# Storing pairs of k-tiles of split weights woven, so that a weight load steps by 8 bytes

## The chip, the cores and the metric

The kernel runs on one core of a Trainium2 chip. The metric is the device time of one execution in microseconds (us).

## What is computed

One decoder layer over 280 token columns: 16 meta tokens, 256 prompt tokens and 8 sample tokens. Nearly all of the arithmetic is in four matrix products in fp32 (D = 2048, DFF = 5632):

```python
z = rmsnorm(x, norm1_g) @ w_in            # 2048 x 16400
x = x + mix @ w_out                       # 2048 x 2048
up = causal_dwconv(rmsnorm(x) @ w_up)     # 2048 x 11264
x = x + (silu(up[..., D_FF:]) * up[..., :D_FF]) @ w_down   # 5632 x 2048
```

Between them stand a short convolution, an mLSTM over 8 heads, gates and norms. Beside the two outputs the kernel returns the new states.

## The kernel before

Activations lie transposed in SBUF: 128 features on the partitions, the tokens along the free axis. Each product is made of strips. A strip is 128 output features; it is accumulated in one PSUM bank (`strip0` to `strip3`, used in turn) over all k-tiles of 128 input features. A strip is made of two or three **units** of at most KU = 8 k-tiles; a unit's weights are one DMA of 128 x 1024 fp32 (512 KB).

fp32 accuracy comes from splitting. `w_hi` is the weight rounded to fp32r, the type with which TensorE makes a product in one pass, and `w_lo` is the rest, `w_raw - w_hi`. The activations are split in the same way (`xh`, `xl` for the norms' outputs, `mh`, `ml` for the mixed heads, `hh`, `hl` for the hidden layer). A unit is 24 matmuls: for each k-tile `w_hi` with `xh` and `w_hi` with `xl` (line 1497), then for each k-tile `w_lo` with `xh` (line 1502). The weights are the stationary operand, so each of these matmuls has its own load of 128 x 128 weights into the array (LDWEIGHTS, shown as engine PEld), and the activations of 264 to 280 token columns stream past them.

The weights go through a ring of RING = 4 slots in each of `w_raw`, `w_hi` and `w_lo`:

- SP (line 379) loads unit u + 4 into `w_raw` when VectorE has made `w_lo` of unit u (`lo_done`).
- ScalarE (line 704, `split_hi`) writes `w_hi` of unit u + 4 when its weights have landed and TensorE has finished unit u (`unit_used`).
- VectorE (line 963, `split_lo`) writes `w_lo` after `hi_done`.
- TensorE waits for `hi_done`, runs the 16 matmuls of the high part, waits for `lo_done`, and runs the 8 of the low part (`unit`, `strip`).

For the first four units VectorE (lines 1009 and 1016), GpSimd (lines 484 and 488) and ScalarE (lines 725 and 726) share that work, in order to start TensorE early (`first_hi`, `first_lo_part`). The order on each engine is written out by hand; loops run over heads, strips and pairs of feature tiles. VectorE also takes every strip out of PSUM (line 972), and VectorE, ScalarE and GpSimd make the convolutions, gates and states.

In each slot k-tile k lies in columns 128 k to 128 k + 127, one word of 4 bytes beside the other.

Of the kernel before, what the change touches and what calls it, by code (L numbers as in the profile page):

```python
# [6 lines left out]
def hybrid_decoder_step(nc, ins, outs, scratch_rows, scratch_v, scratch_q):  # L7
# [10 lines left out]
    f32, f32r = mybir.dt.float32, mybir.dt.float32r  # L18
    ALU, ACT = mybir.AluOpType, mybir.ActivationFunctionType
# [7 lines left out]
    P = 128  # L27
# [12 lines left out]
    NT = TP + NS  # L40
# [24 lines left out]
    KU = 8  # L65
# [37 lines left out]
    with ctx:  # L103
        def sb(name, shape, dt=f32):
            return ctx.enter_context(nc.sbuf_tensor(name, shape, dt))

        def sem(name):
            return ctx.enter_context(nc.semaphore(name))
# [5 lines left out]
        w_raw = sb("w_raw", [P, RING, KU * P])  # L114
        w_hi = sb("w_hi", [P, RING, KU * P], f32r)
        w_lo = sb("w_lo", [P, RING, KU * P], f32r)
# [172 lines left out]
        bank = [ctx.enter_context(nc.psum_tensor(f"strip{i}", [P, 512], f32)) for i in range(RING)]  # L289
# [4 lines left out]
        hi_done = sem("hi_done")  # L294
# [6 lines left out]
        half_hi, first_lo, mp_done, bias_done = sem("half_hi"), sem("first_lo"), sem("mp_done"), sem("bias_done")  # L301
# [55 lines left out]
        def out_of(s):  # L357
            return s + 1 + RING

        def col(c, j):  # L360
            return vecs[:, bass.ds(c * KT + j, 1)]

# [103 lines left out]
        def _(g):  # L466
# [14 lines left out]
            g.memset(gws[:, :, :].bitcast(f32), 0.0).then_inc(gw_split, 1)  # L481
            g.wait_ge(hi_done, 2)
            g.wait_ge(first_lo, 1)
            g.tensor_tensor(w_lo[:, 2, :], w_raw[:, 2, :], w_hi[:, 2, :].bitcast(f32), ALU.subtract)\
             .then_inc(first_lo, 1)
            for i, u in enumerate((1, 3)):
                g.wait_ge(hi_done, i + 3)
                g.tensor_tensor(w_lo[:, u, :], w_raw[:, u, :], w_hi[:, u, :].bitcast(f32), ALU.subtract)\
                 .then_inc(lo_done, 2)

            g.wait_ge(gates_in, 16)
# [152 lines left out]
            for m in range(KT):  # L644
# [5 lines left out]
                if m < NQ:  # L650
                    p = slice(m * Q, (m + 1) * Q)
# [48 lines left out]
        def _(act):  # L700
            def split_hi(u, slot, n16):
                act.wait_ge(unit_landed[slot], n16)
                act.wait_ge(unit_used, u + 1)
                act.activation(w_hi[:, slot, :], w_raw[:, slot, :], ACT.Copy).then_inc(hi_done, 1)  # L704

            def step(n, per, base_u, i):

                u4 = n * per + (base_u + i + RING)
                split_hi(u4, i % RING, n * (16 * per // RING) + 16 * ((base_u + i) // RING + 2))
# [9 lines left out]
            for k in range(KT):  # L719
                act.wait_ge(x_turned, k + 1)  # L720
                act.activation(xh[:, k, :], x_bank[k % 6][:, 0:NT], ACT.Copy, scale=vecs[:, k:k + 1])\
                 .then_inc(xh_done, 1)
                if k == 3:
                    act.wait_ge(unit_landed[0], 16)
                    act.activation(w_hi[:, 0, 0:KU * P // 2], w_raw[:, 0, 0:KU * P // 2], ACT.Copy).then_inc(half_hi, 1)
                    act.activation(w_hi[:, 0, KU * P // 2:], w_raw[:, 0, KU * P // 2:], ACT.Copy).then_inc(hi_done, 1)
                for kept in (k - 2, k) if k % 4 == 3 else ():
                    act.wait_ge(xl_done, kept + 1)
                    act.activation(xres[:, kept, :], x_bank[kept % 6][:, 0:NT], ACT.Copy).then_inc(x_copied, 1)
                if k == 7:  # L730
                    act.wait_ge(hi_done, 2)
                    split_hi(1, 1, 16)
# [227 lines left out]
        def _(v):  # L960
            def split_lo(u, slot):
                v.wait_ge(hi_done, u + 1)
                v.tensor_tensor(w_lo[:, slot, :], w_raw[:, slot, :], w_hi[:, slot, :].bitcast(f32),  # L963
                                ALU.subtract).then_inc(lo_done, 1)

            def step(n, per, base_u, i):
                split_lo(n * per + (base_u + i + RING), i % RING)
# [31 lines left out]
            for k in range(KT):  # L999
                v.wait_ge(xh_done, k + 1)  # L1000
                v.scalar_tensor_tensor(out=xl[:, k, :], in0=x_bank[k % 6][:, 0:NT], scalar=vecs[:, k:k + 1],
                                       in1=xh[:, k, :].bitcast(f32), op0=ALU.mult, op1=ALU.subtract)\
                                        .then_inc(xl_done, 1)
                if k % 2 == 1:
                    v.tensor_copy(xres[:, k - 1, :], x_bank[(k - 1) % 6][:, 0:NT]).then_inc(x_kept, 1)
                if k == 3:
                    v.wait_ge(half_hi, 1)
                    v.wait_ge(hi_done, 1)
                    v.tensor_tensor(w_lo[:, 0, :], w_raw[:, 0, :], w_hi[:, 0, :].bitcast(f32), ALU.subtract)\
                     .then_inc(first_lo, 1)  # L1010
                if k in (3, 11):
                    u = 2 if k == 3 else 3
                    v.wait_ge(unit_landed[u], 16)
                    if k == 11:
                        v.wait_ge(hi_done, 3)
                    v.tensor_scalar(w_hi[:, u, :], w_raw[:, u, :], 1.0, None, ALU.mult).then_inc(hi_done, 1)
            v.wait_ge(lo_done, RING + 4)
            v.wait_ge(ssq_done, 3)
            v.wait_ge(msq_clear, 1)
# [353 lines left out]
        def _(pe):  # L1373
# [43 lines left out]
            def first_hi(s, lo, hi):  # L1417
                c0 = C0 if s == 0 else 0
                for k in range(lo, hi):
                    if s == 0 and k == 0:  # L1420
                        pe.wait_ge(half_hi, 1)
                    elif k % KU == 0 or (s == 0 and k == 4):
                        pe.wait_ge(hi_done, 1 + s + 2 * (k // KU))
                    pe.wait_ge(xl_done, k + 1)
                    w = slice(k % KU * P, (k % KU + 1) * P)
                    for t, xt in enumerate((xh, xl)):
                        mm = pe.matmul(bank[s][:, 0:NT - c0], w_hi[:, 2 * s + k // KU, w], xt[:, k, c0:NT],  # L1427
                                       start=(k == 0 and t == 0), stop=False)
                return mm

            def first_lo_part(s, lo, hi, last=False):
                c0 = C0 if s == 0 else 0
                h = lo // KU
                if h == 0:
                    pe.wait_ge(first_lo, s + 1)
                else:
                    pe.wait_ge(lo_done, RING + 2 * (s + 1))
                for k in range(lo, hi):
                    pe.wait_ge(xh_done, k + 1)
                    mm = pe.matmul(bank[s][:, 0:NT - c0], w_lo[:, 2 * s + h, (k - h * KU) * P:(k - h * KU + 1) * P],  # L1440
                                   xh[:, k, c0:NT], start=False, stop=(last and k == KT - 1))
                return mm

# [7 lines left out]
            turn_x(0, 4)  # L1451
            warm(6)
            first_hi(0, 0, 4)
            turn_x(4, 8)
            first_lo_part(0, 0, 4)
            first_hi(1, 0, 4)
            first_hi(0, 4, 6)
            first_lo_part(0, 4, 8)
            first_hi(0, 6, 8).then_inc(unit_used, 1)
            first_lo_part(1, 0, 4)  # L1460
            turn_x(8, 12)
            first_hi(1, 4, 8)
# [24 lines left out]
            def unit(u, slot, b, k0, kk, rh, rl, c0, c1, first, last, waits=(), frees=1):  # L1487


                pe.wait_ge(hi_done, u + 1)  # L1490
                for k in range(kk):
                    for at_k, sm, value in waits:
                        if at_k == k:
                            pe.wait_ge(sm, value)
                    w = slice(k * P, (k + 1) * P)
                    for t, xt in enumerate((rh, rl)):
                        pe.matmul(bank[b][:, 0:c1 - c0], w_hi[:, slot, w], xt[:, k0 + k, c0:c1],  # L1497
                                  start=(first and k == 0 and t == 0), stop=False)
                pe.wait_ge(lo_done, u + 1 + RING)
                for k in range(kk):  # L1500
                    w = slice(k * P, (k + 1) * P)
                    mm = pe.matmul(bank[b][:, 0:c1 - c0], w_lo[:, slot, w], rh[:, k0 + k, c0:c1],  # L1502
                                   start=False, stop=(last and k == kk - 1))
                if frees:
                    mm.then_inc(unit_used, frees)
# [112 lines left out]
            def out_unit(q, h, waits, frees):  # L1618
                unit(U_B + 2 * q + h, 2 * q + h, q, h * KU, KU, mh, ml, 0, NM, h == 0, h == 1, waits, frees)
# [109 lines left out]
```

## Time and profile before

| | |
|---|---|
| median of 3 runs | 1712.78 us (1712.42 to 1715.47) |
| the profiled execution, own time | 1712.32 us |
| its span, first to last instruction | 1710.6 us |
| TensorE matmul busy (PE) | 1699.2 us, 99% |
| TensorE weight load busy (PEld) | 1692.9 us |
| VectorE (DVE) / ScalarE (ACT) / GpSimd (POOL) busy | 1200.8 / 766.4 / 475.1 us |
| mean granted TensorE clock | 0.998 |

The span is what the trace covers; 1.7 us lie around it. Records of matmuls and loads overlap each other, since a matmul is recorded until its last result is out, so their busy time says only that TensorE never rests. What one matmul costs is the distance from its start to the next one's start, called the pitch below.

### The profile page before, as it was taken

The numbers are of one execution on the slowest core, as the hardware profiler recorded it, in microseconds if no ns is written. First come the engines' busy times: TensorE is split into PE (matmuls) and PEld (weight loads), VectorE is DVE, ScalarE is ACT, GpSimd is POOL, SyncE is SP. The second block draws the span as 40 slices with busy tenths as digits, with TensorE's granted clock in tenths as the row PEclk, the third lists the DMA queues.
The fourth block names the chain that finished last, engine by engine and source line by source line (L and its number), as shares of the span: only waits on it lengthen the run. The fifth ranks groups of instructions, "written<-read, shape, count | busy, mean of one in ns | idle before, by whom it ended". The sixth has DMA issues, their size and how long they took to land.

```text
span 1710.6 us, 37176 instructions
## 1 busy us (share of the span) xinstructions
PE 1699.2 (99%) x13726; PEld 1692.9 (99%) x13726; DVE 1200.8 (70%) x1902; ACT 766.4 (45%) x914; POOL 475.1 (28%) x501
## 2 busy tenths in 40 slices
PE   9999999999999999999999999999999999999997
PEld 8999999999999999999999999999999999999997
DVE  5875958667595766759688877777555777777554
ACT  6545345354443535344444554544333434333443
POOL 4522414242141424215333222222000222222220
PEclk9999999999999999999999999999999999999999
DMA  8787786868778586877866666666666666666663
GB/s 209 176 235 191 203 213 156 223 159 230 188 196 212 155 225 162 232 184 195 192 174 185 186 175 180 179 176 172 183 181 182 180 176 179 174 182 175 182 178 119
DMA packets 591165, 318.80 MB, mean 186 GB/s; under 512 B 17684, under 2 KB 585988, under 8 KB 588988
## 3 DMA queue, kind: packets, MB, share of 16 engines
q1 hardware_dynamic: 578564, 292.99, 63.7%
q10 hardware_dynamic: 10448, 21.57, 4.9%
q0 software_dynamic: 2064, 2.92, 0.8%
q8 instruction: 72, 1.18, 0.3%
q14 instruction: 17, 0.14, 0.0%
HBM read 305.09 MB, written 12.78 MB: 186 GB/s over the span
## 4 chain that ended last, share of the span: by engine, by line
PE 99%; ACT 0%; DVE 0%; POOL 0%; issue 0%; ACTq 0%; POOLq 0%
PE strip L1497 63%; PE strip L1502 32%; PE aux L1375 1%; PE aux L1383 0%; PE strip L1427 0%; PE aux L1555 0%; PE aux L1447 0%; PE strip L1440 0%; PE aux L1585 0%; PE aux L1584 0%; PE aux L1598 0%; PE strip L1375 0%; PE aux L1589 0%; PE aux L1582 0%; PE aux L1590 0%; PE aux L1591 0%
## 5 line engine op out<-in xcount | busy, mean ns | idle before, releaser
L963 DVE TENSOR_TENSOR w_lo<-w_raw,w_hi 128x1024 fp32r<-128x1024 f32 x556 | 718.8, 1296 | 317.6 <-ACT w_hi L704 317.0
L704 ACT ACTIVATE w_hi<-w_raw 128x1024 fp32r<-128x1024 f32 x557 | 586.5, 1059 | 766.0 <-PE strip L1502 730.9
L1497 PE MATMUL strip<-xh,w_hi 128*128 128x268 f32 (+2 forms) x3424 | 863.8, 286 | 0.0
L1497 PE MATMUL strip<-xl,w_hi 128*128 128x268 f32 (+2 forms) x3424 | 862.9, 286 | 0.0
L1497 PEld LDWEIGHTS strip<-xh,w_hi 128*128 128x128 f32 x3424 | 644.9, 188 | 0.2
L1497 PEld LDWEIGHTS strip<-xl,w_hi 128*128 128x128 f32 x3424 | 644.5, 188 | 0.0
L1502 PE MATMUL strip<-xh,w_lo 128*128 128x268 f32 (+2 forms) x3424 | 495.2, 287 | 0.0
L1502 PEld LDWEIGHTS strip<-xh,w_lo 128*128 128x128 f32 x3424 | 451.9, 189 | 0.4 <-DVE w_lo L963 0.4
L1497 PE MATMUL strip<-hh,w_hi 128*128 128x264 f32 x704 | 176.2, 285 | 0.0
L1497 PE MATMUL strip<-hl,w_hi 128*128 128x264 f32 x704 | 174.8, 283 | 0.0
L675 POOL TENSOR_TENSOR gg<-sg,cz 128x264 f32<-128x264 f32 x44 | 57.2, 1301 | 415.1 <-ACT sg L918 415.1
L1497 PEld LDWEIGHTS strip<-hh,w_hi 128*128 128x128 f32 x704 | 132.4, 188 | 0.0
L1497 PEld LDWEIGHTS strip<-hl,w_hi 128*128 128x128 f32 x704 | 132.3, 188 | 0.0
L678 POOL TENSOR_TENSOR hid<-gg,cz 128x264 f32<-128x264 f32 x44 | 73.5, 1671 | 102.2 <-DVE cz L1308 102.2
L1502 PE MATMUL strip<-hh,w_lo 128*128 128x264 f32 x704 | 100.6, 283 | 0.0
L1502 PEld LDWEIGHTS strip<-hh,w_lo 128*128 128x128 f32 x704 | 91.5, 188 | 0.0
L1497 PE MATMUL strip<-ml,w_hi 128*128 128x266 f32 x256 | 64.8, 287 | 0.0
L1497 PE MATMUL strip<-mh,w_hi 128*128 128x266 f32 x256 | 64.7, 287 | 0.0
L615 POOL TENSOR_TENSOR so<-so,sbm 128x266 f32<-128x266 f32 x16 | 20.6, 1287 | 138.9 <-ACT sbm L876 138.9
L972 DVE TENSOR_TENSOR zs<-strip,rbc 128x266 f32<-128x266 f32 x88 | 37.9, 431 | 26.6 <-PE strip L1502 26.6
L606 POOL TENSOR_TENSOR c_st<-c_st,kv 128x512 f32<-128x512 f32 x32 | 52.1, 1628 | 5.4 <-ACT c_st L859 3.4
L1300 DVE SCALAR_TENSOR_TENSOR cz<-zs,vecs,cz 128x256 f32<-128x256 f32 x88 | 42.7, 485 | 12.9 <-DVE cz L1297 1.8
(324 smaller groups left out, 1331.5 us busy)
## 6 DMA issues: line engine op xcount, KB each, us to landing
w_raw<-in_w_in SPq DMA_DIRECT2D x256, 512.0 KB, 4.4
w_raw<-in_w_up SPq DMA_DIRECT2D x176, 512.0 KB, 4.1
w_raw<-in_w_down SPq DMA_DIRECT2D x64, 512.0 KB, 3.9
w_raw<-in_w_out SPq DMA_DIRECT2D x32, 512.0 KB, 4.4
w_raw<-in_w_down SPq DMA_DIRECT2D x32, 384.0 KB, 3.3
out<-c_st ACTq DMA_DIRECT2D x8, 1024.0 KB, 7.1
c_st<-in_state_mlstm_C ACTq DMA_DIRECT2D x7, 1024.0 KB, 10.6
rb<-scratch_rows ACTq DMA_DIRECT2D x8, 270.0 KB, 5.1
```

The source lines that it names most:

```text
L606: g.tensor_tensor(c_p, c_p, kv[:, :, :], ALU.add).then_inc(c_updated, 1)
L615: g.tensor_tensor(so[:, :], so[:, :], sbm[:, :], ALU.mult).then_inc(p_gate, 1)
L675: g.tensor_tensor(gg[:, :], sg[:, :], cz[:, 0, :], ALU.mult).then_inc(gg_done, 1)
L678: g.tensor_tensor(hid[:, :], gg[:, :], cz[:, 1, :], ALU.mult).then_inc(hid_done, 1)
L704: act.activation(w_hi[:, slot, :], w_raw[:, slot, :], ACT.Copy).then_inc(hi_done, 1)
L963: v.tensor_tensor(w_lo[:, slot, :], w_raw[:, slot, :], w_hi[:, slot, :].bitcast(f32), ALU.subtract).then_inc(lo_done, 1)
L972: v.tensor_tensor(out, bank[b][:, c0 - from_c:c0 - from_c + width], rbc[:, c0:c0 + width], ALU.mult).then_inc(evacuated, 1)
L1300: v.scalar_tensor_tensor(out=cz[:, z, 0:SEQ], in0=zs[:, z, 1:1 + SEQ], scalar=wcol[1], in1=cz[:, z, 0:SEQ], op0=ALU.mult, op1=ALU.add)\
L1375: return pe.transpose(out, in_, ident[0:k, 0:k])
L1497: pe.matmul(bank[b][:, 0:c1 - c0], w_hi[:, slot, w], xt[:, k0 + k, c0:c1], start=(first and k == 0 and t == 0), stop=False)
L1502: mm = pe.matmul(bank[b][:, 0:c1 - c0], w_lo[:, slot, w], rh[:, k0 + k, c0:c1], start=False, stop=(last and k == kk - 1))
```

## The change

`w_hi` and `w_lo` are laid out in another order inside a slot. Two neighbouring k-tiles share 256 columns: the even k-tile has the even words, the odd one the odd words. The writers (ScalarE, VectorE, and GpSimd for the first units) read `w_raw` as before and write through a view whose innermost step is two words (`woven`); where they read `w_hi` for the subtraction, they read it through the same view. TensorE's loads of weights take 128 columns two words apart (`wk`). `w_raw` and the DMAs, the activations, the streams past the weights, the semaphores and the order of the instructions are as before: on TensorE and SP each instruction stands where it stood, on ScalarE, VectorE and GpSimd the splitting instructions have the shape 128x4x2x128 in place of 128x1024. The hunks left out are the same edit at ScalarE's first unit and in `first_hi` and `first_lo_part`.

```diff
--- before.py
+++ after.py
@@ -357,6 +357,15 @@
         def out_of(s):
             return s + 1 + RING
 
+        def raw(slot, k0=0, k1=KU):
+            return w_raw[:, slot, k0 * P:k1 * P].rearrange("p (a j n) -> p a j n", j=2, n=P)
+
+        def woven(t, slot, k0=0, k1=KU):
+            return t[:, slot, k0 * P:k1 * P].rearrange("p (a n j) -> p a j n", j=2, n=P)
+
+        def wk(t, slot, k):
+            return t[:, slot, k // 2 * 2 * P + k % 2:(k // 2 + 1) * 2 * P:2]
+
         def col(c, j):
             return vecs[:, bass.ds(c * KT + j, 1)]
 
...
@@ -481,11 +490,11 @@
             g.memset(gws[:, :, :].bitcast(f32), 0.0).then_inc(gw_split, 1)
             g.wait_ge(hi_done, 2)
             g.wait_ge(first_lo, 1)
-            g.tensor_tensor(w_lo[:, 2, :], w_raw[:, 2, :], w_hi[:, 2, :].bitcast(f32), ALU.subtract)\
+            g.tensor_tensor(woven(w_lo, 2), raw(2), woven(w_hi, 2).bitcast(f32), ALU.subtract)\
              .then_inc(first_lo, 1)
             for i, u in enumerate((1, 3)):
                 g.wait_ge(hi_done, i + 3)
-                g.tensor_tensor(w_lo[:, u, :], w_raw[:, u, :], w_hi[:, u, :].bitcast(f32), ALU.subtract)\
+                g.tensor_tensor(woven(w_lo, u), raw(u), woven(w_hi, u).bitcast(f32), ALU.subtract)\
                  .then_inc(lo_done, 2)
 
             g.wait_ge(gates_in, 16)
@@ -701,7 +710,7 @@
             def split_hi(u, slot, n16):
                 act.wait_ge(unit_landed[slot], n16)
                 act.wait_ge(unit_used, u + 1)
-                act.activation(w_hi[:, slot, :], w_raw[:, slot, :], ACT.Copy).then_inc(hi_done, 1)
+                act.activation(woven(w_hi, slot), raw(slot), ACT.Copy).then_inc(hi_done, 1)
 
             def step(n, per, base_u, i):
 
...
@@ -960,7 +969,7 @@
         def _(v):
             def split_lo(u, slot):
                 v.wait_ge(hi_done, u + 1)
-                v.tensor_tensor(w_lo[:, slot, :], w_raw[:, slot, :], w_hi[:, slot, :].bitcast(f32),
+                v.tensor_tensor(woven(w_lo, slot), raw(slot), woven(w_hi, slot).bitcast(f32),
                                 ALU.subtract).then_inc(lo_done, 1)
 
             def step(n, per, base_u, i):
@@ -1006,14 +1015,14 @@
                 if k == 3:
                     v.wait_ge(half_hi, 1)
                     v.wait_ge(hi_done, 1)
-                    v.tensor_tensor(w_lo[:, 0, :], w_raw[:, 0, :], w_hi[:, 0, :].bitcast(f32), ALU.subtract)\
+                    v.tensor_tensor(woven(w_lo, 0), raw(0), woven(w_hi, 0).bitcast(f32), ALU.subtract)\
                      .then_inc(first_lo, 1)
                 if k in (3, 11):
                     u = 2 if k == 3 else 3
                     v.wait_ge(unit_landed[u], 16)
                     if k == 11:
                         v.wait_ge(hi_done, 3)
-                    v.tensor_scalar(w_hi[:, u, :], w_raw[:, u, :], 1.0, None, ALU.mult).then_inc(hi_done, 1)
+                    v.tensor_scalar(woven(w_hi, u), raw(u), 1.0, None, ALU.mult).then_inc(hi_done, 1)
             v.wait_ge(lo_done, RING + 4)
             v.wait_ge(ssq_done, 3)
             v.wait_ge(msq_clear, 1)
...
@@ -1492,14 +1500,12 @@
                     for at_k, sm, value in waits:
                         if at_k == k:
                             pe.wait_ge(sm, value)
-                    w = slice(k * P, (k + 1) * P)
                     for t, xt in enumerate((rh, rl)):
-                        pe.matmul(bank[b][:, 0:c1 - c0], w_hi[:, slot, w], xt[:, k0 + k, c0:c1],
+                        pe.matmul(bank[b][:, 0:c1 - c0], wk(w_hi, slot, k), xt[:, k0 + k, c0:c1],
                                   start=(first and k == 0 and t == 0), stop=False)
                 pe.wait_ge(lo_done, u + 1 + RING)
                 for k in range(kk):
-                    w = slice(k * P, (k + 1) * P)
-                    mm = pe.matmul(bank[b][:, 0:c1 - c0], w_lo[:, slot, w], rh[:, k0 + k, c0:c1],
+                    mm = pe.matmul(bank[b][:, 0:c1 - c0], wk(w_lo, slot, k), rh[:, k0 + k, c0:c1],
                                    start=False, stop=(last and k == kk - 1))
                 if frees:
                     mm.then_inc(unit_used, frees)

```

## Rows read from the trace of the kernel before

**Rows 1.** The page, parts 1 and 2: busy us, share, instructions; TensorE's clock.
```profile
PE 1699.2 (99%) x13726; PEld 1692.9 (99%) x13726; DVE 1200.8 (70%) x1902; ACT 766.4 (45%) x914; POOL 475.1 (28%) x501
...
PEclk9999999999999999999999999999999999999999
```

**Rows 2.** The page, part 4: shares of the chain that ended last, by engine.
```profile
PE 99%; ACT 0%; DVE 0%; POOL 0%; issue 0%; ACTq 0%; POOLq 0%
```

**Rows 3.** The page, part 5: groups of strip matmuls, for their counts.
```profile
L1502 PE MATMUL strip<-xh,w_lo 128*128 128x268 f32 (+2 forms) x3424 | 495.2, 287 | 0.0
...
L1502 PE MATMUL strip<-hh,w_lo 128*128 128x264 f32 x704 | 100.6, 283 | 0.0
...
L1497 PE MATMUL strip<-ml,w_hi 128*128 128x266 f32 x256 | 64.8, 287 | 0.0
```

**Rows 4.** Windows: stretch, length, each engine busy (count), clock, DMA share, GB/s.
```profile
129.00:147.00 18.00, 18.00 (x142) 18.00 (x142) 9.14 (x12) 6.37 (x6) 2.13 (x7) 1.00 0.96 227
156.00:190.00 34.00, 34.00 (x277) 34.00 (x277) 27.28 (x36) 18.84 (x29) 20.01 (x19) 1.00 0.52 133
195.00:229.00 34.00, 34.00 (x280) 34.00 (x279) 22.88 (x34) 13.00 (x15) 10.05 (x10) 1.00 0.90 240
826.00:916.00 90.00, 90.00 (x729) 90.00 (x728) 70.79 (x96) 36.90 (x46) 36.83 (x48) 1.00 0.75 188
925.00:1175.00 250.00, 250.00 (x2034) 250.00 (x2033) 198.74 (x385) 126.31 (x129) 58.34 (x42) 1.00 0.62 178
1185.00:1305.00 120.00, 120.00 (x993) 120.00 (x992) 62.47 (x62) 47.75 (x45) 0.00 (x0) 1.00 0.64 184
```

**Rows 5.** Timeline: start us, length us, engine, line, shape; loads and half-rate matmuls.
```profile
13.55 0.47 PEld L1375 LDWEIGHTS strip<-ident,x_tok 128*128 128x128 f32 x4
...
90.89 0.31 PEld L1585 LDWEIGHTS aux<-pt,v 128*128 128x128 f32 x2
91.00 0.41 PE L1585 MATMUL aux<-pt,v 128*128 128x144 f32 x2
...
92.70 0.53 PEld L1598 LDWEIGHTS aux<-sel,sacc 128*128 128x128 f32 x4
```

**Rows 6.** Lines L1375, L1447, L1497, L1585: ns min/median/max, first and last start.
```profile
L1375 PEld LDWEIGHTS strip<-ident,x_tok x4: 139/140/142, 13.5 to 13.9; 128*128 128x128 f32 x4
...
L1447 PEld LDWEIGHTS aux<-xh,gws x16: 167/168/174, 27.9 to 31.7; 128*104 128x104 f32 x16
...
L1497 PEld LDWEIGHTS strip<-xh,w_hi x3424: 186/188/193, 33.0 to 1566.4; 128*128 128x128 f32 x191
...
L1585 PEld LDWEIGHTS aux<-pt,v x32: 191/192/192, 90.9 to 793.2; 128*128 128x128 f32 x32
```

**Rows 7.** Timeline of PE: consecutive matmuls of one shape.
```profile
1300.11 0.28 PE L1497 MATMUL strip<-hh,w_hi 128*128 128x264 f32 x1
1300.22 0.29 PE L1497 MATMUL strip<-hl,w_hi 128*128 128x264 f32 x1
1300.36 0.28 PE L1497 MATMUL strip<-hh,w_hi 128*128 128x264 f32 x1
1300.47 0.29 PE L1497 MATMUL strip<-hl,w_hi 128*128 128x264 f32 x1
```

**Rows 8.** The page, part 5: splitting on VectorE and ScalarE, and a short eviction.
```profile
L963 DVE TENSOR_TENSOR w_lo<-w_raw,w_hi 128x1024 fp32r<-128x1024 f32 x556 | 718.8, 1296 | 317.6 <-ACT w_hi L704 317.0
L704 ACT ACTIVATE w_hi<-w_raw 128x1024 fp32r<-128x1024 f32 x557 | 586.5, 1059 | 766.0 <-PE strip L1502 730.9
...
L972 DVE TENSOR_TENSOR zs<-strip,rbc 128x266 f32<-128x266 f32 x88 | 37.9, 431 | 26.6 <-PE strip L1502 26.6
```

**Rows 9.** Lines L963 and L1016 by themselves: ns min/median/max, first and last start.
```profile
L963 DVE TENSOR_TENSOR w_lo<-w_raw,w_hi x556: 1181/1224/2891, 31.6 to 1689.8; 128x1024 fp32r<-128x1024 f32 x186
...
L1016 DVE TENSOR_SCALAR w_hi<-w_raw x2: 680/682/683, 13.0 to 21.5; 128x1024 fp32r<-128x1024 f32 x2
```

More of the change, by code:

```diff
@@ L724, in _ @@
                     act.wait_ge(unit_landed[0], 16)
-                    act.activation(w_hi[:, 0, 0:KU * P // 2], w_raw[:, 0, 0:KU * P // 2], ACT.Copy).then_inc(half_hi, 1)
-                    act.activation(w_hi[:, 0, KU * P // 2:], w_raw[:, 0, KU * P // 2:], ACT.Copy).then_inc(hi_done, 1)
+                    act.activation(woven(w_hi, 0, 0, KU // 2), raw(0, 0, KU // 2), ACT.Copy).then_inc(half_hi, 1)
+                    act.activation(woven(w_hi, 0, KU // 2), raw(0, KU // 2), ACT.Copy).then_inc(hi_done, 1)
                 for kept in (k - 2, k) if k % 4 == 3 else ():
@@ L1424, in first_hi @@
                     pe.wait_ge(xl_done, k + 1)
-                    w = slice(k % KU * P, (k % KU + 1) * P)
                     for t, xt in enumerate((xh, xl)):
-                        mm = pe.matmul(bank[s][:, 0:NT - c0], w_hi[:, 2 * s + k // KU, w], xt[:, k, c0:NT],
+                        mm = pe.matmul(bank[s][:, 0:NT - c0], wk(w_hi, 2 * s + k // KU, k % KU), xt[:, k, c0:NT],
                                        start=(k == 0 and t == 0), stop=False)
@@ L1439, in first_lo_part @@
                     pe.wait_ge(xh_done, k + 1)
-                    mm = pe.matmul(bank[s][:, 0:NT - c0], w_lo[:, 2 * s + h, (k - h * KU) * P:(k - h * KU + 1) * P],
+                    mm = pe.matmul(bank[s][:, 0:NT - c0], wk(w_lo, 2 * s + h, k - h * KU),
                                    xh[:, k, c0:NT], start=False, stop=(last and k == KT - 1))
```

## The prediction, made before the changed kernel was run

> **What bounds the kernel now.** I read the page first. TensorE is busy for 99% of the span and its clock is granted in full in every slice [rows 1], which is its level of 2.4 GHz. The chain of work that ended last is TensorE's own for 99% [rows 2]. So the span is a sum of matmul pitches (start to start), and the change can act in two ways: it alters the pitch, or it slows a writer of weights so much that TensorE must wait.
>
> The strips have 13,248 matmuls. The lines of the loops show 3424 + 704 + 256 = 4384 for one of the three products of a k-tile [rows 3], so 13,152, and the first units add 4 x 24 = 96. For their pitch I asked for windows that hold strips and little else [rows 4]. A window also counts the matmul or two that began before it, so I add one matmul's length, 0.28 us [rows 7], before I divide: 128.8 ns for 280 columns (129:147), 123.8 and 122.4 for 268 (156:190 and 195:229), 123.8 and 123.0 for 266 (826:916 and 925:1175), 121.1 for 264 (1185:1305). At one column per cycle of 2.4 GHz these streams take 116.7, 111.7, 110.8 and 110.0 ns. So every strip matmul costs 11 to 13 ns more than its stream, about 11.8 on average. That is 13,248 x 11.8 = 156 us of the span, and the only part of it that a layout of weights can touch.
>
> **What the excess is.** Three readings.
> (a) It is not the other engines or the DMAs: of the two windows with 268 columns the one with a DMA share of 0.52 has 123.8 ns and the one with 0.90 has 122.4 [rows 4].
> (b) It is not the length of the load. A load of 104 columns is recorded at 168 ns and one of 128 at 188 [rows 6], so 20/24 = 0.83 ns per column, and 128 columns take 107 ns. Four loads whose matmuls stream only 8 columns follow each other in (0.53 - 0.19)/3 = 0.113 us [rows 5, 6]. So a load fits into the 121 to 129 ns of a pitch, but with only some 10 ns to spare.
> (c) Where the stream runs at two cycles per column, the excess is hardly there, though the loads are as many. Two matmuls of 144 columns: loads (0.31 - 0.19) = 0.12 us apart, against 2 x 144/2.4 = 120 ns. Transposes of 128 columns: (0.47 - 0.14)/3 = 0.11 us, against 107 [rows 5, 6]. I take 2.5 ns, and it may be 0 to 5.
> Besides, gaps between matmuls of one shape in one strip are uneven: 0.11, 0.14, 0.11 us [rows 7].
>
> My reading, an inference and not shown by a row: the load of the next weights and the stream of the present matmul read SBUF at the same time, and when both want the same part of it the stream stalls. At full rate the stream has no free cycles to make up for it; at half rate it has. In bytes per partition the stream now advances at 4 / 0.417 = 9.6 B/ns and the load at 4 / 0.83 = 4.8 B/ns, so the stream overtakes the load again and again within a matmul.
>
> **The change part by part.**
> *Loads.* 13,248 loads step by 8 bytes instead of 4. If a load keeps its 0.83 ns per column, it now advances at 9.6 B/ns, as fast as the stream. Then the two keep a fixed distance. If they collide at the start, one stall puts them apart for the rest of the matmul. So the stalls should mostly go. At best the pitch falls to the stream plus 2.5 ns: 9.3 ns less for each, 13,248 x 9.3 = 123 us. The floor set by the load itself, 107 to 113 ns, is just reached at 264 columns (110 + 2.5). I take 8 of the 9.3 ns, since one or two stalls at the start of a matmul should remain: 13,248 x 8 = 106 us. The other end: the trace before has no load that steps, so nothing excludes that a step costs time. A load of twice as many SBUF lines could double the conflicts (+9.3 ns), or double its length (second and fourth rival).
>
> *Writers.* 557 splits on ScalarE (1059 ns) and 556 on VectorE (1296 ns) now write with a step of two words, and VectorE reads `w_hi` so [rows 8]. VectorE's subtraction costs (1224 - 431)/(1024 - 266) = 1.05 ns per element, with its median of 1224 ns [rows 9] and an eviction of 266 elements at 431 [rows 8]: one element per step, nothing packed that a stride could break. I cost them at nothing. What hides them is the ring: ScalarE waited 730.9 us for TensorE before its splits, and VectorE 317.0 us for ScalarE [rows 8], and a unit's weights are due only when three more units of 24 x 0.123 = 2.95 us have run. With pitches shorter by 8 ns a unit lasts 24 x 0.115 = 2.76 us. VectorE's 1200.8 us [rows 1] then fill 75% of 1606 us, so it does not become the bound.
>
> *Start.* VectorE makes `w_hi` of units 2 and 3 in 0.68 us each for 1024 elements [rows 9], faster than one element per 1.05 ns (1.07 us). A step may take this away: 2 x 0.4 = 0.8 us, bounded by nothing and by twice that, at a place where GpSimd and TensorE wait for it. I add 1 us.
>
> *Unchanged.* DMAs, instruction order and waits. The DMA share is 0.96 at worst while states are loaded [rows 4]; units that come 7% sooner press on that place, and `w_raw` may land late there. Eight such stretches at up to 1 us give 0 to 8 us; I take 1.
>
> **Sum.** Against the profiled execution's own 1712.3 us (the median of the runs is 1712.8, the same within 0.03%): -106 + 1 + 1 = -104, so **1608 us**.
>
> **A rule that speaks against it.** By rows, the excess is 11 to 13 ns beside full-rate streams and 0 to 5 beside half-rate ones, and this is what I build on. The Trainium skill, "TensorE: Matmul & The Clock Gate", section "Step-by-step: what each phase is for", says that TensorE has two independent read ports into SBUF and that loading the next weights takes no read bandwidth from the running matmul. By that there is no conflict to remove. "Advanced Engine Details and Errata", section "SBUF Cachelines", adds that lines are 16 bytes and that two hits per line suffice for full speed: a step of 8 bytes of fp32 has just two. By both the time would stay at 1712; no run here shows a stepped load yet.
>
> **The rivals.**
> 1. *The excess is a fixed cost of changing weights at full rate and the layout does not matter.* Pitch 121 to 129 as before, 1712 to 1713 us. For it: the excess is near 12 ns at 264 and at 280 columns [rows 4]. Against it: the uneven gaps [rows 7], and 266 columns costing 123.8 in one stage and 123.0 in another [rows 4]. The rules above give the same time. 18%.
> 2. *Slower: conflicts grow with the lines that a load touches.* 128 columns now span 1024 bytes instead of 512. Twice the conflicts is +9.3 ns, 13,248 x 9.3 = +123, so 1836 us. It decides as soon as the stalls per matmul exceed today's; at half of that growth the time is 1774. For it: a faster load has less idle time between its reads. Against: only if the fixed distance does not hold. 21%.
> 3. *Slower: the writers become the bound.* If a stepped write or read took two steps per element, VectorE's 556 subtractions would take 1.07 us more each: 1200.8 + 595 = 1796 us of work, more than the span. With some idle time left, 1800 to 1850. ScalarE at 766.4 + 590 would still fit. For it: only that no large stepped write is in the trace. 5%.
> 4. *Slower: the load takes twice as long.* 2 x 107 + 6 = 220 ns per matmul instead of 123: 13,248 x 97 = +1285, so about 3000 us. For it: the load has only some 10 ns to spare. 6%.
>
> **How the numbers follow.** My forecast has 50%; its own range goes from 1585 (all 123 us, with the small losses at nothing) to 1695 (a seventh of it). The predicted time is its 1608. The range that should hold 8 in 10 must reach the first two rivals: 1585 to 1840. Outside lie the fourth rival, some of the third and the upper part of the second. A measurement of this kernel tells 0.2%, about 3.4 us, from no change. Faster: 50%. Within 0.2%: the first rival, 18%. Slower: 21 + 5 + 6 = 32%.
>
> **What would show it.** In the profile of the changed kernel: windows in the same stages with about 115 ns per matmul instead of 123, gaps in a strip that are even, loads still recorded near 188 ns, splits near 1059 and 1224 ns, TensorE still at 99%. A load recorded at 290 ns or so would be the fourth rival. Splits near 2.3 us with TensorE waiting for `w_lo` would be the third. Gaps above 123 ns with loads at 188 would be the second. Unchanged pitches to within 0.3 ns would be the first. The prediction is wrong if the excess is not a conflict between load and stream, or if equal speed makes the conflict permanent instead of ending it.

## The result, and the profile after

The changed kernel takes 1735.99 us (median of 4 runs, 1735.41 to 1737.38) where the one before takes 1712.9. The ratio is 1.0131, with a 95% interval of 1.0119 to 1.0143: it is slower by 23 us, and clear of the 0.2% that a measurement can tell.

The page of the changed kernel: the clock and TensorE's share are as in [rows 1], ScalarE's busy time is up by 51 us, and VectorE's (-1.6 us) and GpSimd's (+3.5 us) hardly move.

```profile
PE 1723.2 (99%) x13726; PEld 1716.8 (99%) x13726; DVE 1199.2 (69%) x1902; ACT 817.1 (47%) x914; POOL 478.6 (28%) x501
...
L713 ACT ACTIVATE w_hi<-w_raw 128x1024 fp32r<-128x1024 f32 x557 | 638.3, 1153 | 746.2 <-PE strip L1508 701.3
```

TensorE's own waits after (engine and line that waited, for whom: us in total, times, longest). This is all of them, none is for weights, and the kernel before has the same three (2.1, 1.2 and 0.3 us); so the time went into the pitch:

```profile
PE aux L1392 <- POOL a L484: 2.1, 1, 2.1
PE aux L1700 <- DVE rfs L999: 1.2, 1, 1.2
PE aux L1689 <- ACT sqs L906: 0.3, 1, 0.3
```

Windows of the changed kernel in the stages of [rows 4], moved to where those stages now lie (stretch, length, busy and count of PE, PEld, DVE, ACT, POOL, clock, DMA share, GB/s):

```profile
132.00:148.00 16.00, 16.00 (x125) 16.00 (x125) 7.36 (x11) 6.07 (x6) 1.36 (x7) 1.00 0.98 221
158.00:192.00 34.00, 34.00 (x276) 34.00 (x275) 27.06 (x37) 19.86 (x30) 20.15 (x19) 1.00 0.53 136
198.00:232.00 34.00, 34.00 (x276) 34.00 (x275) 22.43 (x33) 13.97 (x15) 10.06 (x10) 1.00 0.88 238
835.00:925.00 90.00, 90.00 (x722) 90.00 (x722) 68.58 (x96) 39.69 (x45) 40.01 (x47) 1.00 0.75 185
935.00:1185.00 250.00, 250.00 (x1989) 250.00 (x1988) 194.59 (x379) 131.50 (x126) 56.46 (x42) 1.00 0.61 174
1200.00:1320.00 120.00, 120.00 (x979) 120.00 (x978) 60.67 (x60) 51.00 (x45) 0.00 (x0) 1.00 0.63 181
```

With one matmul's 0.28 us added as in the prediction, the pitches are 130.2 ns at 280 columns (128.7 before by [rows 4], where the prediction wrote 128.8), 124.2 at 268 in both stages (123.8 and 122.4), 125.0 and 125.8 at 266 (123.8 and 123.0), and 122.9 at 264 (121.1). So the cost is uneven, from 0.4 to 2.8 ns. The mean over the starts of all strip matmuls in the two traces rises from 123.4 to 125.1 ns, that is by 1.74 ns, and 13,248 x 1.74 = 23 us. The span grew by 24.1 us (1710.6 to 1734.7); the other 1.2 us lie at the start, see below. The loads are recorded 8 ns longer than in [rows 6]. VectorE's subtractions keep their median of [rows 9] within 2 ns and its two copies within 4 ns (ns min/median/max):

```profile
L1504 PEld LDWEIGHTS strip<-xh,w_hi x3424: 193/196/203, 34.3 to 1588.6; 128*128 128x128 f32 x191
...
L972 DVE TENSOR_TENSOR w_lo<-w_raw,w_hi x556: 1181/1226/2884, 33.0 to 1713.9; 128x1024 fp32r<-128x1024 f32 x186
...
L1025 DVE TENSOR_SCALAR w_hi<-w_raw x2: 682/686/689, 14.2 to 22.7; 128x1024 fp32r<-128x1024 f32 x2
```

### The profile page after: what moved, and what is told of

The parts are those of the page before. It is cut to its first block, busy times and chain, and to the rows that moved or that the text cites. A ratio compares the mean times of both kernels' runs of the same rounds, so it can differ in the third digit from the quotient of the medians.

```text
span 1734.7 us, 37176 instructions
## 1 busy us (share of the span) xinstructions
PE 1723.2 (99%) x13726; PEld 1716.8 (99%) x13726; DVE 1199.2 (69%) x1902; ACT 817.1 (47%) x914; POOL 478.6 (28%) x501
## 4 chain that ended last, share of the span: by engine, by line
PE 94%; DVE 2%; ACT 1%; issue 1%; DMA 1%; POOL 0%; DVEq 0%; ACTq 0%; POOLq 0%
PE strip L1504 61%; PE strip L1508 31%; DVE w_lo L972 1%; PE aux L1384 1%; PE aux L1561 0%; DMA rb<-scratch_rows 0%; DMA scratch_rows<-rows 0%; ACT sq_junk L748 0%; PE aux L1591 0%; PE aux L1590 0%; PE aux L1604 0%; PE aux L1597 0%; PE aux L1588 0%; PE aux L1596 0%; PE aux L1595 0%
## 5 line engine op out<-in xcount | busy, mean ns | idle before, releaser
L713 ACT ACTIVATE w_hi<-w_raw 128x1024 fp32r<-128x1024 f32 x557 | 638.3, 1153 | 746.2 <-PE strip L1508 701.3
L1504 PE MATMUL strip<-xh,w_hi 128*128 128x268 f32 (+2 forms) x3424 | 878.2, 290 | 0.0
L1504 PE MATMUL strip<-xl,w_hi 128*128 128x268 f32 (+2 forms) x3424 | 875.7, 288 | 0.0
L1504 PEld LDWEIGHTS strip<-xl,w_hi 128*128 128x128 f32 x3424 | 674.5, 197 | 0.0
L1504 PEld LDWEIGHTS strip<-xh,w_hi 128*128 128x128 f32 x3424 | 671.4, 196 | 0.2
L1508 PEld LDWEIGHTS strip<-xh,w_lo 128*128 128x128 f32 x3424 | 458.3, 196 | 0.3 <-DVE w_lo L972 0.3
L1504 PEld LDWEIGHTS strip<-hh,w_hi 128*128 128x128 f32 x704 | 137.9, 196 | 0.0
L1504 PEld LDWEIGHTS strip<-hl,w_hi 128*128 128x128 f32 x704 | 137.5, 195 | 0.0
L1504 PEld LDWEIGHTS strip<-ml,w_hi 128*128 128x128 f32 x256 | 50.6, 198 | 0.0
```

Source lines behind the costliest of these rows:

```text
L713: act.activation(woven(w_hi, slot), raw(slot), ACT.Copy).then_inc(hi_done, 1)
L1504: pe.matmul(bank[b][:, 0:c1 - c0], wk(w_hi, slot, k), xt[:, k0 + k, c0:c1], start=(first and k == 0 and t == 0), stop=False)
L1508: mm = pe.matmul(bank[b][:, 0:c1 - c0], wk(w_lo, slot, k), rh[:, k0 + k, c0:c1], start=False, stop=(last and k == kk - 1))
```

## The experiments

All start from the kernel before, except the one with the writers, which starts from the changed one. Of each edit the lines that matter are shown; the same edit is made where `w_lo` is loaded, and a stepped or step-0 load also in the first four units. None of these kernels computes the layer: they leave out work or multiply other data. Differences below are between a kernel's median and that of the kernel before in the same session (1713.5 to 1714.5 us).

### Which half of the change costs

Loads alone:

```diff
+        def wk(t, slot, k):
+            return t[:, slot, k // 2 * 2 * P + k % 2:(k // 2 + 1) * 2 * P:2]
-                        pe.matmul(bank[b][:, 0:c1 - c0], w_hi[:, slot, w], xt[:, k0 + k, c0:c1],
+                        pe.matmul(bank[b][:, 0:c1 - c0], wk(w_hi, slot, k), xt[:, k0 + k, c0:c1],
```

> Only the loads step by 8 bytes; the writers store plain as before (so each load takes every second word of two k-tiles, and the products are other ones). If the 23 us come from the stepped loads, it shows all of them: 1735 to 1737 us, loads at 196 ns, ScalarE's split back at 1059 ns. If they come from the stepped writes on ScalarE and VectorE that disturb TensorE's reads, it is back at 1712 to 1714 us with loads at 188 ns. A mixture would lie between.

Writers alone (the changed kernel with `wk` reading 128 neighbouring columns):

```diff
-            return t[:, slot, k // 2 * 2 * P + k % 2:(k // 2 + 1) * 2 * P:2]
+            return t[:, slot, k * P:(k + 1) * P]
```

> The complement: the writers store woven, the loads are plain again (the products are other ones). If the loads are the cause: 1712 to 1714 us, loads at 188 ns, ScalarE's split still at 1156 ns, which the ring hides. If the writes are the cause: 1735 us.

Loads alone: 1736.31 us, ratio 1.0127 (1.011 to 1.0144). Writers alone: 1713.93 us, ratio 1.0 (0.999 to 1.0009). All of the cost in the pitch is in the loads. The woven write does make ScalarE's split longer (1146 ns instead of 1059), and the ring hides it. Page of the kernel with loads alone, then of the one with writers alone (the last columns: busy us, mean ns, idle before it):

```profile
L1498 PEld LDWEIGHTS strip<-xh,w_hi 128*128 128x128 f32 x3424 | 671.4, 196 | 0.2
L707 ACT ACTIVATE w_hi<-w_raw 128x1024 fp32r<-128x1024 f32 x557 | 586.5, 1059 | 792.2 <-PE strip L1502 755.6 <-DMA w_raw<-in_w_in 18.7 <-issue 7.3
```

```profile
L1504 PEld LDWEIGHTS strip<-xh,w_hi 128*128 128x128 f32 x3424 | 644.9, 188 | 0.2
L713 ACT ACTIVATE w_hi<-w_raw 128x1024 fp32r<-128x1024 f32 x557 | 634.4, 1146 | 723.2 <-PE strip L1508 681.2 <-DMA w_raw<-in_w_in 20.9 <-issue 8.3
```

### A longer step, and none

```diff
+            return t[:, slot, k // 4 * 4 * P + k % 4:(k // 4 + 1) * 4 * P:4]     # step 16 bytes
+            return t[:, slot, k * P:k * P + 1].broadcast_to([P, P])              # step 0
```

> Loads step by 16 bytes, one word of each 16, writers plain (other products). Theory A, the cost grows with the number of 16-byte lines that a load touches (32, 64, now 128): recorded load at least 196 + 16 = 212 ns, excess above the stream another 3 to 4 ns or more, 1780 us or slower; if one hit per line costs the load a full second access, its length doubles and the time is above 2500 us. Theory B, any step costs the same fixed amount: 1735 to 1740 us. Theory C, the length of the path through SBUF banks matters by chance of addresses: anything from 1700 to 1760 us.

> All 128 columns of a load are the same word (step 0; other products): the load touches a single line. Theory A (load and stream disturb each other by the lines the load reads): the excess over the stream falls from 11.8 to near 2.5 ns, 1590 to 1620 us. Rival (a fixed cost of full-rate matmuls with a load each): 1712 us, no change.

Step of 16 bytes: 3183.44 us, ratio 1.8569 (1.8538 to 1.86). The window of 1695 to 2170 (266 columns) and the loads of that kernel:

```profile
1695.00:2170.00 475.00, 475.00 (x2030) 475.00 (x2030) 200.25 (x386) 124.93 (x127) 57.85 (x42) 1.00 0.32 94
```

```profile
L1498 PEld LDWEIGHTS strip<-xh,w_hi 128*128 128x128 f32 x3424 | 1132.7, 331 | 0.2
```

The load is 331 - 188 = 143 ns longer, and the pitch is 475.28/2030 = 234 ns here, and 233 and 234 ns in the stages with 280 and 268 columns: the load has become the bound. With one word used of each 16 bytes, the loads follow each other in 234 ns where plain ones did in 0.113 us [rows 5]; with two words used (8 bytes) a load is recorded 8 ns longer. The Trainium skill, "Advanced Engine Details and Errata", section "SBUF Cachelines", says that two hits per line suffice and that a line for each access costs; the cliff between 8 and 16 bytes agrees, but two hits were not quite free for loads.

Step 0: 1698.34 us, ratio 0.991 (0.9893 to 0.9926), 16 us less where the theory behind my prediction wanted 95 to 125. A load that touches a single line leaves the excess at some 10.5 ns. The window of 918 to 1160 gives 242.28/1991 = 121.7 ns, against 123.0 before and a stream of 110.8:

```profile
918.00:1160.00 242.00, 242.00 (x1991) 242.00 (x1991) 194.55 (x380) 123.50 (x126) 57.61 (x41) 1.00 0.62 180
```

So most of the excess does not go with the lines that the load reads. That theory (A in the expectation) fell here, and so did the rival beside it, which had no change at all.

### Streams that stay in one place

```diff
-                                  xt[:, k0 + k, c0:c1],
+                                  xt[:, k0 + k, c0:c0 + 1].broadcast_to([P, c1 - c0]),
```

> Plain loads; in the strips' matmuls of the loops each stream reads one word over and over (step 0; other products). With the load's lines already shown to matter little (step 0 there took 16 us off), what remains of the excess of about 11 ns per matmul is either the stream's own reading of SBUF, in which case the pitch falls to the stream plus 2.5 ns and the time to 1590 to 1600 us, or a fixed cost of one load and one full-rate matmul each, in which case it stays within 1695 to 1715 us.

> The same with loads that step by 8 bytes. If stepped loads cost by conflicts with the stream's reads, the step adds nothing here: equal to the run with plain loads and one-word streams, within 3 us, though the load may still be recorded at 196 ns. If the stepped load by itself is longer and holds up the next matmul, it adds the same 22 us as with real streams.

Plain loads: 1618.16 us, ratio 0.9443 (0.9427 to 0.9459), 95 us less. Stepped loads: 1651.58 us, ratio 0.9636 (0.962 to 0.9652), 33 us more than the plain ones. The plain one is slower than the 1590 to 1600 us expected, though its pitch is as expected (below), because TensorE, now faster, waits for others: 8.8 us for `w_lo` (22 times) and once 4.4 us for `hl`, where TensorE in the kernel before waits for neither, and the granted clock is 0.97 in the stretch with that longest wait (1120:1235). So read the pitches rather than the total. Two windows of each, with 280 and with 266 columns (plain, then stepped):

```profile
127.00:141.00 14.00, 14.00 (x120) 14.00 (x119) 6.24 (x9) 4.51 (x5) 2.62 (x7) 1.00 1.00 232
...
785.00:870.00 85.00, 85.00 (x753) 85.00 (x752) 70.22 (x98) 38.84 (x48) 39.92 (x50) 1.00 0.82 204
```

```profile
130.00:145.00 15.00, 15.00 (x128) 15.00 (x127) 6.80 (x9) 4.71 (x5) 2.73 (x7) 1.00 0.96 221
...
798.00:885.00 87.00, 87.00 (x741) 87.00 (x739) 70.26 (x97) 37.50 (x48) 39.61 (x49) 1.00 0.78 197
```

Plain: 119.0 and 113.3 ns, which is the stream plus 2.4 at either width. And the gaps, uneven in [rows 7], are even now (timeline of that kernel):

```profile
900.10 0.28 PE L1497 MATMUL strip<-xl,w_hi 128*128 128x266 f32 x1
900.21 0.28 PE L1497 MATMUL strip<-xh,w_hi 128*128 128x266 f32 x1
900.33 0.28 PE L1497 MATMUL strip<-xl,w_hi 128*128 128x266 f32 x1
```

So nearly all of the excess needs a stream that moves through SBUF. No run has such a stream without a load beside it; what the runs do show is that the excess stays nearly whole when the load shrinks to one line, or to a quarter of its length (below). With stepped loads the pitch is 119.4 ns at 280 columns, the same as with plain ones, but 117.8 at 266. Neither outcome that I had written down came alone: where the stream plus 2.4 ns is longer than 117.8 ns the step costs nothing, and where it is shorter the stepped load is a floor of 117.8 ns. For plain loads that floor was 0.113 us [rows 5]. In the changed kernel the mean pitches are 122.9 ns and more, above the floor. Single pitches vary, but only 379 of 13,174 in the trace before are under 118 ns, and raising those to 117.8 ns would cost 0.4 us. So its 23 us come another way.

### Lines or columns of a load

```diff
+                        m = P if k == 0 and t == 0 and first else 96
-                        pe.matmul(bank[b][:, 0:c1 - c0], w_hi[:, slot, w], xt[:, k0 + k, c0:c1],
+                        pe.matmul(bank[b][0:m, 0:c1 - c0], w_hi[:, slot, w][:, 0:m], xt[:, k0 + k, c0:c1],
```

and the same for `w_lo`; then with `wk`, and with 32 and 64 in place of 96.

> Plain loads of 96 columns in place of 128 in all but the first and last matmul of a strip (a quarter of each product is left out). 96 columns are 27 ns shorter to load. If the length of the load holds up the next matmul, the time falls by 100 us or more; if the excess is not set by the load's length, it stays at 1705 to 1715 us, as the gates' loads of 104 columns suggest.

> The same loads of 96 columns with a step of 8 bytes. Theory L (a stepped load of 128 columns is just too long for the gap: about 8 ns are added to a load that had some 10 ns to spare): with 27 ns more room the step costs nothing, equal to the plain 96-column run within 3 us. Theory N (the number of lines or conflicts matters): 48 lines where the plain one has 24, so three quarters of the 22 us, 15 to 18 us above the plain 96-column run.

> Plain loads of 32 columns in all but the first and last matmul of a strip (three quarters of each product are left out): 8 lines of 16 bytes per load. If the cost goes with the load's lines at the 0.6 us per line seen so far, 24 lines less give 14 to 16 us: 1697 to 1700 us, and the rest of the excess is the stream's own. If the excess is a conflict with the load after all, it falls with the load's length to a quarter: 1620 to 1640 us.

> Loads of 64 columns with a step of 8 bytes (half of each product is left out): 32 lines, as many as the plain load of 128 columns. If lines decide: 1710 to 1716 us, like before. If a step costs something of its own, whatever the lines: above 1720 us. If columns decide: 1705 us or less.

Ordered by the lines of 16 bytes that one load touches:

| load | lines | recorded load | time | difference | ratio, 95% interval |
|---|---|---|---|---|---|
| 128 columns, step 0 | 1 | 188 ns | 1698.34 us | -16.0 us | 0.9893 to 0.9926 |
| 32 columns, plain | 8 | 108 ns | 1700.18 us | -13.4 us | 0.9907 to 0.994 |
| 96 columns, plain | 24 | 162 ns | 1709.80 us | -3.7 us | 0.9968 to 0.9987 |
| 128 columns, plain (before) | 32 | 188 ns | 1713.5 us | 0 | |
| 64 columns, step 8 bytes | 32 | 138 ns | 1711.82 us | -1.7 us | 0.9979 to 0.9998 |
| 96 columns, step 8 bytes | 48 | 167 ns | 1724.28 us | +10.8 us | 1.0045 to 1.0079 |
| 128 columns, step 8 bytes | 64 | 196 ns | 1736.31 us | +22.0 us | 1.011 to 1.0144 |

The time goes with the lines, 0.5 to 0.7 us for each line more or less, and neither with the columns nor with the recorded length: the load of 96 stepped columns is shorter than the plain one of 128 and costs 11 us more, and 64 stepped columns cost about what 128 plain ones do. 0.6 us over 13,248 matmuls is 0.045 ns per line. Two limits of this table: in every load of it but the first, the lines are also the distance that the load covers, divided by 16 bytes, so the runs do not tell the count of lines from that distance; and the shorter loads also make their matmuls write fewer rows of the bank. The load of 96 stepped columns in the page of its kernel:

```profile
L1499 PEld LDWEIGHTS strip<-xl,w_hi 128*96 128x96 f32 x3424 | 571.6, 167 | 0.1
```

### What in the stream costs

```diff
+    return t[:, 0:2, :].rearrange('p k n -> p (k n)')[:, o:o + n]            # k-tile 0 always; o = 0, 16 or 32 words for xh, xl
+    return t[:, k, 0:g].unsqueeze(1).broadcast_to([P, n // g, g])            # one line; g = 4, or 2 at 266 columns
+    return t[:, k, 0:n // g].unsqueeze(1).broadcast_to([P, g, n // g])       # a half twice; a seventh 7 times at 266 columns
```

> Plain loads; every strip matmul streams k-tile 0 of its operand instead of its own k-tile (other products), so the stream starts at the same address in every matmul. Theory D (what is left of the excess is one access per 16 bytes of the stream, wherever it lies): same mean pitch as before, 1705 to 1720 us, and uneven gaps may stay. Theory E (it depends on where stream and load lie to each other): the gaps in a unit become even and their mean moves by more than 1 ns, so the time moves by more than 13 us to either side.

> As the run with one k-tile, with the streams from xh and xl starting 64 bytes further. Theory D: equal to that run within 3 us. Theory E: differs from it by more than 5 us.

> As the run with one k-tile, with the streams from xh and xl starting 128 bytes further. Theory D: equal within 3 us. Theory E: differs by more than 5 us.

> Plain loads; each stream reads the first 4 words (2 words at 266 columns) of its k-tile again and again, so it stays in one line of 16 bytes but does not have step 0 (other products). If it is distinct lines that cost, the pitch is that of the step-0 streams, stream plus 2.5 ns, 1618 us. If each fetch costs whatever its line, it stays at 1700 us or above, more so in the stages with 266 columns, which have twice the groups.

> Plain loads; streams read the first half of their columns twice, at 266 columns the first seventh seven times (other products). The number of passages from line to line is as before, the number of different lines 33 or 10 instead of 66 to 70. If passages cost (the stream's own rate of fetching): 1700 to 1716 us. If different lines cost: about 1665 us in the stages with halves, and near the stream plus 3 or 4 ns at 266 columns.

One line, over and over: 1617.77 us, ratio 0.9436 (0.942 to 0.9452), the same as step 0. Half twice or a seventh seven times: 1760.43 us, ratio 1.0272 (1.0255 to 1.0289), slower than before though far fewer different lines are read. The windows of that kernel give 32.28/256 = 126.1 ns at 268 columns and 260.28/2016 = 129.1 ns at 266:

```profile
160.00:192.00 32.00, 32.00 (x256) 32.00 (x255) 26.35 (x36) 17.32 (x26) 19.36 (x18) 1.00 0.51 134
...
945.00:1205.00 260.00, 260.00 (x2016) 260.00 (x2015) 197.07 (x383) 124.34 (x127) 59.00 (x42) 1.00 0.59 168
```

So it is the passing from line to line that costs, not how many different ones there are, and jumping back costs on top of it, though the time expected for that (1700 to 1716 us) was missed: six jumps at 266 columns cost 6 ns (123.0 before), one at 268 some 2 to 3 ns, and one at 280, where the half ends with a line, 0.5 ns (16.28/126 = 129.2). Whether the loss is one for each passage or one for each stream that moves, these widths (66 to 70 lines) cannot tell.

Always k-tile 0: 1720.36 us (+5.9, ratio 1.004, 1.0026 to 1.0054), starting 64 bytes further 1715.01 us (+0.5, not to be told from nothing), 128 bytes further 1725.02 us (+10.5, ratio 1.0066, 1.005 to 1.0083). Theory D (addresses do not matter) allowed 3 us between the three, theory E (they do) asked for more than 5, and for 13 us and even gaps in the first. The shift of 64 bytes moved the time by 5.4 us and that of 128 by 4.7, the first kernel by 5.9, and its gaps at 266 columns stayed uneven (117 to 128 ns). So addresses matter, by 0.4 to 0.8 ns per matmul, which is more than D allows, but they do not make the main part of the excess.

## Why the prediction was wrong

**What bounds the kernel** was right. TensorE bounds it at full clock, each matmul costs 11 to 13 ns more than its stream, and the change acts on that through the loads alone.

**"What the excess is", reading (c) and what I inferred from it, is the step that failed.** I saw that the excess is nearly absent where the stream runs at two cycles per column, and concluded that it is a conflict between load and stream. The observation fits as well a stream that at full rate cannot pass from line to line without a loss, and that is what the runs show: with streams in one line the excess is 2.4 ns with unchanged loads, with loads in one line it is still some 10.5 of the 11.8 ns, and with loads of a quarter of the columns 10.8. The load's share is 16 us (step 0) of the 156 us, where I took 123 us for removable. No row of the trace before separates the two, since every full-rate matmul there has both a moving stream and a load of 104 or 128 columns. The inference should have stood against a rival of its own, "the stream alone", which was missing from my list.

**Reading (a)** was worded more widely than its rows. They speak of the DMAs alone; of the two stretches the one with the longer pitch also has busier engines [rows 4]. The trace before settles it: the strip matmuls of 268 columns take 123.4 ns while VectorE works and 122.8 while it rests (3503 and 1171 of them), those of 266 columns 122.9 and 123.5 (3530 and 696). So only 0.6 ns goes with VectorE's work, and not always with the same sign; for ScalarE and GpSimd it is no more at any width.

**"The two keep a fixed distance"** was wrong as well. If it were so, the small share that the load does have would have gone. It more than doubled instead: 31 lines less took 16 us off, 32 lines more put 22 us on.

**The second rival** came true in kind: conflicts grow with the lines a load touches. I had priced it on the wrong base. Doubling 9.3 ns gave +123 us; by the runs the load's share is 16 us, or 19 us at 0.6 us for each of 32 lines, and 32 lines more cost 22 us. Its chance was 21%. Why a line costs this is open.

**Writers at nothing** was right, and shown: ratio 1.0. ScalarE's split did grow, by 87 ns in that run and 94 ns in the changed kernel, which I had not seen coming; the ring covers it. The third rival is out.

**Start:** VectorE's two copies kept their speed (682 to 686 ns), so the reason for my 1 us was wrong. TensorE reaches the first strip of the loop 1.3 us later (34.3 against 33.0 us; 33.9 with loads alone, 32.9 with writers alone). That is neither the loads nor the copies: ScalarE's very first split already starts at 11.66 against 10.46 us (11.24 and 10.34 in those two runs), before TensorE's first load of split weights. What delays it is not shown. So the 1 us came out near its size by luck.

**The first rival**, a fixed cost that no layout changes, is out as well: the layout moved the time by 1.3%. The 1 us that the prediction gives to late DMAs could not be tested, since no unit came sooner.

**The fourth rival** did not come at 8 bytes. It came at 16, at 3183 us.

**The rule that spoke against it.** By independent read ports (the Trainium skill, "TensorE: Matmul & The Clock Gate", "Step-by-step: what each phase is for") a load's layout should not touch the running matmul. It does, by about 0.045 ns per line, which for 64 lines is 2.9 ns or 2% of a pitch; but the rule was nearer to the truth than my reading, which had it at 9 ns per matmul.

The time lies inside the wide range, on the other side from the forecast, and only because that range was drawn to hold the second rival too; that is no merit of the mechanism.

## What to carry to other kernels

When a cost shows only in rows that hold two suspects at once (here a moving full-rate stream and a load beside it), find a row or a run that changes only one of them before pricing a gain on either. In a kernel like this one, keep fp32 weights plain in SBUF: at a step of 8 bytes the loads cost 1.3% of the time, and at 16 bytes 86%. None of the runs gives a layout that beats the kernel before; those that are faster leave out work or read other data.

## What the runs showed of the hardware that I had not expected

- A full-rate fp32r matmul with its own load costs the stream plus 2.4 ns only when the stream stays within one line (113.3 ns at 266 columns, 119.0 at 280). Streaming real columns costs 9.7 ns more (123.0 and 128.7). Half-rate matmuls hardly show it (at most some 3 ns, [rows 5, 6]). Why passing from line to line costs this stays open, and so does the mechanism by which a line of the load costs 0.045 ns. The latter needs a stream that passes lines: at 280 columns in one line the stepped load added nothing.
- The shortest pitch that a load of 128 fp32r columns allows: 0.113 us plain, 117.8 ns at a step of 8 bytes, 234 ns at 16.
- ScalarE's copy of 1024 elements takes 1059 ns with plain and 1146 ns with woven output; VectorE's subtraction of as many, with woven output and one woven input, takes the same as plain (median 1226 and 1224 ns).
